# Forgetting tile of a two-layer encoder: 32 columns split, low parts packed beside the high ones

## The reference

```python
def hybrid_mixer(u, w_in, ...):
    proj = u @ w_in                                   # 1024 x 1796
    qa, ka, va, us, qc, kc, vc, fc = jnp.split(proj, IN_SPLITS, axis=-1)
    ya = swa_sink_attention(qa, ka, va, swa_sinks, cos, sin)
    yb = s5_mixer(us, ...)
    yc = fox_attention(qc, kc, vc, fc, fox_f_bias)
    y = jnp.concatenate([rms_norm(ya, ga), rms_norm(yb, gb), rms_norm(yc, gc)], axis=-1)
    return y @ w_out

def fox_attention(q, k, v, f_logit, f_bias):
    logf = jax.nn.log_sigmoid(f_logit + f_bias)       # FOX_HEADS = 4 columns
    cum = jnp.cumsum(logf, axis=1)
    ...                                               # cum biases the scores
```

## Time and profile before

| | before |
|---|---|
| median of 3 runs | 1875.31 us (1874.92 to 1875.57) |
| profiled execution, its own time | 1874.11 us |
| its span, first to last instruction | 1872.3 us |
| mean granted TensorE clock | 0.999 |
| PE / PEld busy | 1856.3 us (99%) / 1534.4 us (82%) |
| DVE / ACT / POOL busy | 986.5 / 710.3 / 202.3 us |
| loads in flight | 101 GB/s mean |

### The profile page before, as it was taken

The page is one execution under the profiler, slowest core; times in us unless marked ns, Lnnn a source line. Parts: engine busy times, 40 slices in busy tenths (PEclk is TensorE's granted clock), DMA queues, the critical chain, the costliest instruction groups (busy, mean ns, idle before and its releaser), DMA issues.

```text
span 1872.3 us, 25256 instructions
## 1 busy us (share of the span) xinstructions
PE 1856.3 (99%) x9480; PEld 1534.4 (82%) x9480; DVE 986.5 (53%) x1350; ACT 710.3 (38%) x1115; POOL 202.3 (11%) x420
## 2 busy tenths in 40 slices
PE   9999999999999999999999999999999999999998
PEld 7888888888678888888888888889886888888887
DVE  6664433387757544432476544325877574444323
ACT  5333332255755333322253333223666453333321
POOL 3832000013100000000047200000130000000000
PEclk9999999999999999999999999999999999999999
DMA  6335343343223333343333443333511313333331
GB/s 197 101 103 146 95 119 93 85 144 102 57 68 91 98 93 101 95 121 94 100 93 99 108 132 113 107 95 104 161 51 53 113 57 101 93 98 114 97 93 45
DMA packets 332013, 188.61 MB, mean 101 GB/s; under 512 B 7028, under 2 KB 327512, under 8 KB 330904
## 3 DMA queue, kind: packets, MB, share of 16 engines
q1 hardware_dynamic: 325992, 168.60, 31.3%
q0 software_dynamic: 5824, 18.79, 3.3%
q10 hardware_dynamic: 112, 0.05, 0.0%
HBM read 175.72 MB, written 11.67 MB: 100 GB/s over the span
## 4 chain that ended last, share of the span: by engine, by line
PE 96%; DVE 2%; ACT 2%; issue 0%; DVEq 0%; ACTq 0%
PE ps L595 19%; PE ps L597 18%; PE ps L596 18%; PE ps L804 8%; PE ps L805 8%; PE ps L806 8%; PE ps L652 2%; PE ps L654 2%; PE ps L659 2%; PE ps L990 1%; PE ps L764 1%; PE ps L763 1%; PE ps L765 1%; PE ps L625 1%; PE ps L636 1%; PE ps L627 1%
## 5 line engine op out<-in xcount | busy, mean ns | idle before, releaser
L1677 DVE TENSOR_TENSOR wl<-raw,wh 128x1024 fp32r<-128x1024 f32 (+1 forms) x260 | 344.4, 1325 | 729.3 <-ACT wh L1175 728.0
L595 PE MATMUL ps<-xh,wh 128*128 128x512 f32 x1536 | 606.1, 395 | 2.2 <-ACT vc L1398 2.2
L597 PE MATMUL ps<-xh,wl 128*128 128x512 f32 x1536 | 598.2, 389 | 0.0
L596 PE MATMUL ps<-xl,wh 128*128 128x512 f32 x1536 | 597.9, 389 | 0.0
L1175 ACT ACTIVATE wh<-raw 128x1024 fp32r<-128x1024 f32 (+1 forms) x260 | 295.8, 1139 | 621.4 <-PE ps L806 324.6
L595 PEld LDWEIGHTS ps<-xh,wh 128*128 128x128 f32 x1536 | 288.4, 188 | 66.1 <-issue 4.8
L597 PEld LDWEIGHTS ps<-xh,wl 128*128 128x128 f32 x1536 | 288.3, 188 | 60.5
L596 PEld LDWEIGHTS ps<-xl,wh 128*128 128x128 f32 x1536 | 288.5, 188 | 60.0 <-issue 1.9
L804 PE MATMUL ps<-Hh,wh 128*128 128x512 f32 x638 | 248.4, 389 | 0.0
L806 PE MATMUL ps<-Hh,wl 128*128 128x512 f32 x638 | 248.2, 389 | 0.0
L805 PE MATMUL ps<-Hl,wh 128*128 128x512 f32 x638 | 248.2, 389 | 0.0
(11 more groups left out here) (390 smaller groups left out, 2020.0 us busy)
## 6 DMA issues: line engine op xcount, KB each, us to landing
raw<-in_ffn_gate SPq DMA_DIRECT2D x88, 512.0 KB, 3.8
raw<-in_ffn_up SPq DMA_DIRECT2D x88, 512.0 KB, 3.8
raw<-in_ffn_down SPq DMA_DIRECT2D x64, 704.0 KB, 4.5
raw<-in_w_in SPq DMA_DIRECT2D x28, 512.0 KB, 4.1
raw<-in_w_out SPq DMA_DIRECT2D x16, 512.0 KB, 3.6
xrow<-in_x SPq DMA_DIRECT2D x4, 512.0 KB, 7.2
ssm_t<-evict POOLq DMA_DIRECT2D x8, 256.0 KB, 3.6
ssm_v<-evict POOLq DMA_DIRECT2D x8, 256.0 KB, 3.5
```

The lines of the kernel that those rows point to most:

```text
L595: pe.matmul(bank, w_tile(True, slot, kw), xh[:, kx, :], start=first, stop=False)
L596: pe.matmul(bank, w_tile(True, slot, kw), xl[:, kx, :], start=False, stop=False)
L597: return pe.matmul(bank, w_tile(False, slot, kw), xh[:, kx, :], start=False, stop=last)
L1677: V.tensor_tensor(w_low(slot, k0, nk), raw[:, slot4, 0:nk - k0, :], w_high(slot, k0, nk).bitcast(F32), ALU.subtract).then_inc(w_split, 1)
```

## The change

Only the last 32 of the 128 columns of the fc tile are split. Their low parts go into the high tile's own memory, in front of them: columns 64 to 95 hold the low parts, 96 to 127 the high ones. One product with these 64 weight columns gives high and low by the same input in rows 32 to 63 and 0 to 31 of the bank; a second with `xl` gives the same again. So there are two products of 64 weight columns per k in place of three of 128 (the low part is now multiplied by `xl` too). `forget` scales both row groups and adds them, three operations in place of one. Loads stay as they were.

```diff
+FC_ROWS = 2 * (P - CUM0)
+def narrow_from(s, i):
+
+    return CUM0 if s % 3 == 1 and i in (2, 3) else 0
...
+                narrow = TILE["fc"] if s % 3 == 1 else None
+
+                def product(u, high, xt, k, cols_h, start, stop):
+
+                    if u != narrow:
+                        return pe.matmul(ps[u][:, cols_h], w_tile(high, cols[u][1], k), xt[:, k, cols_h], start=start, stop=stop,
+                                         skip_group_check=True)
+                    if high:
+                        return pe.matmul(ps[u][0:FC_ROWS, cols_h], w_tile(True, cols[u][1], k)[:, P - FC_ROWS:P], xt[:, k, cols_h],
+                                         start=start, stop=stop, skip_group_check=True)
...
-                            bank = ps[u][:, :]
-                            pe.matmul(bank, w_tile(True, cols[u][1], k), xh[:, k, :], start=(k == 0), stop=False,
-                                      skip_group_check=True)
-                            pe.matmul(bank, w_tile(False, cols[u][1], k), xh[:, k, :], start=False, stop=False,
-                                      skip_group_check=True)
+                            product(u, True, xh, k, whole, k == 0, False)
+                            product(u, False, xh, k, whole, False, False)
...
-                            mm = pe.matmul(ps[u][:, :], w_tile(True, cols[u][1], k), xl[:, k, :], start=False, stop=(k == KD - 1),
-                                           skip_group_check=True)
+                            mm = product(u, True, xl, k, whole, False, k == KD - 1)
...
-                act.activation(w_high(slot, k0, nk), raw[:, slot4, 0:nk - k0, :], ACT.Copy).then_inc(w_hi, 1)
+                act.activation(w_high(slot, k0, nk)[:, :, c0:P], raw[:, slot4, 0:nk - k0, c0:P], ACT.Copy).then_inc(w_hi, 1)
...
-                V.tensor_tensor(w_low(slot, k0, nk), raw[:, slot4, 0:nk - k0, :],
-                                w_high(slot, k0, nk).bitcast(F32), ALU.subtract).then_inc(w_split, 1)
+                dst = w_high(slot, k0, nk)[:, :, P - FC_ROWS:CUM0] if c0 else w_low(slot, k0, nk)
+                V.tensor_tensor(dst, raw[:, slot4, 0:nk - k0, c0:P],
+                                w_high(slot, k0, nk)[:, :, c0:P].bitcast(F32), ALU.subtract).then_inc(w_split, 1)
...
-                    r = slice(CUM0, P)
                     complete(m)
-                    mlink(V.tensor_tensor(full[r, 1, :], ps[bank_of(m)[0]][r, :], rstd[r, :], ALU.mult))
+                    r, bank = slice(CUM0, P), ps[bank_of(m)[0]]
+                    mlink(V.tensor_tensor(full[r, 1, :], bank[0:FC_ROWS // 2, :], rstd[0:FC_ROWS // 2, :], ALU.mult))
+                    mlink(V.tensor_tensor(full[r, 0, :], bank[FC_ROWS // 2:FC_ROWS, :], rstd[FC_ROWS // 2:FC_ROWS, :], ALU.mult))
+                    mlink(V.tensor_tensor(full[r, 1, :], full[r, 1, :], full[r, 0, :], ALU.add))
                     free(m)
```

More of the change, by code:

```diff
@@ L611, in first_four @@
                 order = FIRST if s else FIRST0
+                narrow = TILE["fc"] if s % 3 == 1 else None
[6 more added lines that the diff above has]
+                                         start=start, stop=stop, skip_group_check=True)
+                whole = slice(0, SEQ)
                 if s:
@@ L623, in first_four @@
                                     pe.wait_ge(w_split, cols[u][0] + RAW_SLOTS + 1)
-                                bank = ps[u][:, cols_h]
-                                pe.matmul(bank, w_tile(True, cols[u][1], k), xh[:, k, cols_h], start=(first and k == 0), stop=False,
-                                          skip_group_check=True)
-                                pe.matmul(bank, w_tile(False, cols[u][1], k), xh[:, k, cols_h], start=False, stop=False,
-                                          skip_group_check=True)
+                                product(u, True, xh, k, cols_h, first and k == 0, False)
+                                product(u, False, xh, k, cols_h, False, False)
                             if first and k == 0:
@@ L635, in first_four @@
                             for u in ALL4:
-                                pe.matmul(ps[u][:, cols_h], w_tile(True, cols[u][1], k), xl[:, k, cols_h],
-                                          start=False, stop=False, skip_group_check=True)
+                                product(u, True, xl, k, cols_h, False, False)
                 for step, (ks, us_) in enumerate(order):
@@ L1169, in ssm_functions, with split, split_unit @@
                 act.activation(identb[:, :], ident[:, :], ACT.Copy).then_inc(act_c, 1)
-            def split(n, q, slot4, slot, nk, occupant=2, k0=0):
+            def split(n, q, slot4, slot, nk, occupant=2, k0=0, c0=0):
                 act.wait_ge(landed[slot4], q * 16 + 16)
                 act.wait_ge(unit_done, n + SPLIT_SLOTS + 1 - occupant)
-                act.activation(w_high(slot, k0, nk), raw[:, slot4, 0:nk - k0, :], ACT.Copy).then_inc(w_hi, 1)
-            def split_unit(n, slot, nk=KD, occupant=2, k0=0):
-                split(n, n // 4, n % 4, slot, nk, occupant, k0)
+                act.activation(w_high(slot, k0, nk)[:, :, c0:P], raw[:, slot4, 0:nk - k0, c0:P], ACT.Copy).then_inc(w_hi, 1)
+            def split_unit(n, slot, nk=KD, occupant=2, k0=0, c0=0):
+                split(n, n // 4, n % 4, slot, nk, occupant, k0, c0)
             def split_ahead(s, i):
                 n, slot, k0, k1, since = ahead(s, i)
-                split_unit(n, slot, k1, since, k0)
+                split_unit(n, slot, k1, since, k0, narrow_from(s, i))
             def root(total, width, r, lns, ln_count, done):
@@ L1672, in ssm_inverse, with low, low_unit @@
                     link(V.tensor_scalar(nsinks[r, :, :], mine, -1.0, None, ALU.mult))
-            def low(n, slot4, slot, nk, k0=0):
+            def low(n, slot4, slot, nk, k0=0, c0=0):
                 dve.wait_ge(w_hi, n + 1)
-                V.tensor_tensor(w_low(slot, k0, nk), raw[:, slot4, 0:nk - k0, :],
-                                w_high(slot, k0, nk).bitcast(F32), ALU.subtract).then_inc(w_split, 1)
-            def low_unit(n, slot, nk=KD, k0=0):
-                low(n, n % 4, slot, nk, k0)
+                dst = w_high(slot, k0, nk)[:, :, P - FC_ROWS:CUM0] if c0 else w_low(slot, k0, nk)
+                V.tensor_tensor(dst, raw[:, slot4, 0:nk - k0, c0:P],
+                                w_high(slot, k0, nk)[:, :, c0:P].bitcast(F32), ALU.subtract).then_inc(w_split, 1)
+            def low_unit(n, slot, nk=KD, k0=0, c0=0):
+                low(n, n % 4, slot, nk, k0, c0)
             def low_ahead(s, i):
                 n, slot, k0, k1, _ = ahead(s, i)
-                low_unit(n, slot, k1, k0)
+                low_unit(n, slot, k1, k0, narrow_from(s, i))
             def x_low(s, d):
```

## The result

The changed kernel takes 1879.73 us (median of 17 executions, 1877.08 to 1882.92), the kernel before in the same sittings 1875.26 us. The ratio is 1.0025, 95% interval 1.0019 to 1.0031: slower by 4.5 us, where 12.3 us were predicted and 1881.6 us was the low end. (Two of the 17 executions of before took 2196 and 4824 us; without them its median is 1875.23 us.) The executions spread over 5.8 us, the other 15 of before over 3.3 us.

The account below looks back on a forecast made before the run. PE was taken as the bound, without slack against DVE from 403 to 444 us. -3.7 + 13.1 + 2.9 = +12.3 us on 1875.3 gave 1887.6 us, own range 1885.2 to 1889.6, wider range 1881.6 to 1890.5.

Parts of the forecast that it names:

- What comes on PE: changes of weight width: Forgetting tile's products: switching between 128 and 64 weight columns drains PE, 38 runs at 0.345 us, +13.1 us.
- the price of a run: Time a run of narrow products among wide ones costs PE beside its own pace, taken as 0.345 us.
- Rival 1: Narrow split-type products on PE cause no drain, their loads run ahead: -0.8 us, 1874.5 us; chance 8%.
- The term for DVE: Two more forgetting operations on DVE, 1.44 us a layer, delay PE at the third score item: +2.9 us.
- The sign that it rested on: PE idling for ACT's exp at the third score item's mask product (L961), once a layer, 0.4 us in all.
- The saving on PE: Forgetting tile's third product per k, with low weights, goes: 1.85 us per layer, -3.7 us in both.
- switches: The drains on PE at entering and leaving runs of narrow products in the forgetting tile: +13.1 us.
- the forecast's own range: Whole kernel: 1885.2 to 1889.6 us, from 38 x 0.05 us for the runs and 0.5 us for DVE; forecast's chance 60%.

Follow-up runs that it names:

- e2: The changed kernel with its narrow products in plain float32 instead of the split type: 1908.37 us, one execution.
- e4: The kernel before with three linked forgetting operations on DVE in place of one, all products as before: 1880.2 us, ratio 1.0024.
- e7: The changed kernel with two forgetting operations on DVE (ACT copies the low rows) and the forget sum's scan later on DVE: 1873.99 us, 0.9997 of before.
- e12: The kernel before with only two moves, the forget sum's scan ahead of the fifth rotation and PE's sum of squares two k later: 1875.25 us, ratio 1.0003.
- e6: The changed kernel with seven throwaway products of 384 columns in PE's wait ahead of the third score item, in each layer: 1877.42 us.
- e10: The kernel of e7 with PE's sum of squares two k later: 1873.46 us, 0.9992 of the kernel before; run again, 1874.32 us, 0.9996.

## Why the prediction was wrong

**What failed.** The step "What comes on PE: changes of weight width", +13.1 us in a sum of +12.3. It read the price of a run rightly from rows 3 and 5, as e2 confirms (0.34 us). It controlled for a break and a semaphore with rows 6, and concluded "So it is the width". But each narrow product in its rows was plain float32. The control, wide and plain float32, showed only that the type alone brings no drain; no row had a narrow product of the split type. Its price there is zero: starts 0.23 us apart. The Trainium skill, TensorEngine Tiling (Array Packing), Key Properties, has the drain at a change of tiling mode; e2 shows such a drain for plain float32, and the changed kernel shows none for fp32r with 64 weight columns. Rival 1 was this case and had 8%, with the difference of type named in it.

**The term for DVE** was right in place and nearly in size: 1.44 us a layer predicted, 1.54 and 1.52 measured between the squares and the third item, of which 0.1 is the uncovered weight load of the squares' product. e4 has 1.46 without that wait. The sign that it rested on was misread, though: the 0.4 us of rows 9 are idling of the weight loads, and PE itself stood still for 0.08 us there (L933 ends at 440.56 + 3.79 = 444.35, L961 starts at 444.43). That there was no slack holds all the same: with the scan moved, e7 and e12 need 0.2 us less for the third column.

**The saving on PE** was priced rightly (the narrow products keep the pace), but it does not arrive: 1.85 us a layer became 0.26 and 0.62. The prediction called PE itself the bound in this stretch because its products had no hole; that didn't say how near the next wait was. Had the drains come, PE would have been later than DVE at the sum of squares, as in e2, where it doesn't idle there; without them it is earlier, and waits. Rival 1 took the saving whole; it should have asked what is late next once PE gets faster. Its 1874.5 us would otherwise be: - 0.9 + 3.1 = +2.2, about 1877.5 us, which is e6.

**What the prediction did not have** is the clock. It foresaw a longer wait at the third item and priced it as its length. The rest up to 1879.7 us, 2.3 us in the median, are products at a granted clock of 0.50, the level of 1.2 GHz, in some executions and layers and not in others; most of the spread comes from this.

| | predicted | measured |
|---|---|---|
| third product gone | -3.7 | -0.9 after the waits |
| switches | +13.1 | 0 |
| DVE's operations | +2.9 | +3.1 |
| lower clock | none | +2.3 |
| sum | +12.3 | +4.5 |

One slip of arithmetic changes nothing: with 38 x 0.05 us and 0.5 us the forecast's own range ends at 1890.0 us, not at 1889.6.

**What stays open.** Why exactly a fall comes in one layer and not in the other; how products of further types with 64 weight columns behave; and whether e10 beats the kernel before.

## What to carry to other kernels

A product taken from a saturated TensorE is worth its pace only as far as the next rendezvous with another engine: look for the wait with the least slack behind it before counting it. Two small vector operations a layer on such a chain cost 3.1 us here, and 5.4 us together with the lower clock; 22 TensorE products fewer saved 0.9. And a price read from neighbours holds only for what they share with the new instruction: if every example has two properties together, here 64 columns and plain float32, name both, and give the other one a real chance.

## What the runs showed of the hardware

- fp32r products with 64 weight columns, writing rows 0 to 63, among fp32r products with 128: weight loads run ahead, starts 0.23 us apart at 512 columns and 0.12 at 256. The same in plain float32: the load starts 0.31 us after the product ahead of it, and a run costs 0.34 us beside its own pace (e2).
- A plain float32 product of 512 columns with 64 weight columns has a pace of 0.86 us, one of the split type 0.23 (e2, changed kernel).
- An idle time of 1.1 us on TensorE, behind 3.8 us of products on 64 columns of input, was followed by 3 us and more at a granted clock of 0.50; filled with seven throwaway products, by 1.00.
- What such a wait of 1.1 us cost on top of its length was nothing in one layer and 3.0 us in the other, in one execution (e4).
